# Stick-breaking attention in a transformer block: column sums on VectorE ahead of the product with minus ones

## The chip, the cores and the metric

The kernel runs on one core of a Trainium2 chip. The metric is the time of the whole program on the device, in microseconds; the program computes two transformer blocks of 512 tokens by 1024 channels in one launch, and the change touches one of the four mixers of the first.

## The reference

The stick-breaking mixer has 4 heads of 64 dimensions over 512 tokens. For a query i and the keys j before it:

```python
z = einsum('bqhd,bkhd->bhqk', q_blk, k) * scale
strict = kpos[None, :] < (t0 + arange(Q_BLOCK))[:, None]
log_1m = where(strict, log_sigmoid(-z), 0.0)
rem = cumsum(log_1m, axis=3, reverse=True) - log_1m
a = where(strict, exp(log_sigmoid(z) + rem), 0.0)
out = einsum('bhqk,bkhd->bqhd', a, v)
```

log_sigmoid(-z) is minus softplus(z), so log a is z minus the sum of softplus(z) over the key itself and all later keys that are still before the query.

## The kernel before, in words

Scores are held with keys on the partitions and queries on the free axis, in blocks of 128 keys. Key block kt has the queries from kt*128 on: 512, 384, 256 and 128 columns for kt = 0 to 3. They lie one behind another in the tile `sb_sp` (`sb_sp_t` in the profile), 1280 columns for each of two heads, at `SB_OFF` = 0, 512, 896, 1152. The heads go in two pairs (0, 1) and (2, 3), and the key blocks of a pair from the last to the first.

Three kinds of steps stand in the list `ORDER`, which all engines walk in the same order, each doing its own part of each step:
- `("sb_scores", pair, kt)`: TensorE multiplies keys by queries into a PSUM bank z(h,kt) and adds the causal mask through an identity (L1040 to L1052). ScalarE computes ln(1+exp(-|z|)) in three activations (L1479 to L1481). VectorE adds max(z, 0) and writes the softplus to `sb_sp` (L1963), which hands the bank back.
- `("sb_exp", pair, kt)`: TensorE takes the same bank over as r(h,kt) and adds to z the sum over later keys, with a minus sign (L1053 to L1064): for each later block j a product of the 128x128 matrix of minus ones (`sbm[:, 1]`) with the whole of block j's softplus, and for its own block a product with a triangular matrix (`sbm[:, 0]`). ScalarE takes the exponential into `sb_a` (L1489).
- `("sb_pv", pair)`: TensorE multiplies values by `sb_a`; ScalarE copies the result to `y[:, 6 + pair]`.

The core of the TensorE step is

```python
for j in range(NT - 1, kt, -1):
    mm(out[:, (j - kt) * P:w], sbm[:, 1], sb_sp[:, h % 2, SB_OFF[j]:SB_OFF[j] + T - j * P],
       False, False, skip_group_check=True)
last = mm(out[:, 0:w], sbm[:, 0], sb_sp[:, h % 2, SB_OFF[kt]:SB_OFF[kt] + w], False, True,
          skip_group_check=True)
```

All of it is in float32, where one matmul shows as two records in the profile. Matmuls are recorded at line L709 (a helper), transposes at L993.

These steps are woven by `plan()` between the attention steps of another mixer (`att_scores`, `att_norm`, `att_turn`, `att_pv` with units `("mla", head, query block)`), a projection in float32 halves (`fmk`, tiles `h_hi`, `h_lo`, `w_hi_t`, `w_lo_t`) and the output norms `("norm", ("y", g))` with `y_out(g)`. In the order of the list, what matters here is:

```
216 sb_scores 0,1   218 att_pv(0,1)  219 att_scores(2,0)  223 sb_exp 0,2  224 att_turn(0,3)
231 sb_scores 0,0   237 att_norm(2,2)  238 sb_exp 0,1   239 att_turn(2,1)  240 y_out 0
243 att_scores(2,3)  246 sb_scores 1,3   249 sb_exp 0,0   252 att_pv(2,2)   253 sb_pv 0
258 sb_scores 1,1   261 sb_scores 1,0   262 y_out 2   263 sb_exp 1,1   264 fmk wout k 0-1
265 sb_exp 1,0      266 fmk wout k 2    267 sb_pv 1   then y_out 3 and the rest of wout
```

(an attention step names one of its two heads.) A `y_out` on VectorE is six operations of 512 columns (L1572, L1636, L1640, twice). PSUM has eight banks, taken in the order in which they were filled; a taker waits until the last user has read it. GpSimd splits each weight tile into a high part (L2140) and a low part (L2142, `w_lo_t<-w_raw,w_hi_t`), as slots come free.

Of the kernel before, what the change touches and what calls it, by code (L numbers as in the profile page):

```python
# [19 lines left out]
ALU = mybir.AluOpType  # L20
# [5 lines left out]
P = 128  # L26
T = 512
NT = T // P
# [283 lines left out]
SEMAPHORES = """x_in0 x_in1 x_in2 x_in3 x_back ones_set r_cols mask_in mixer_in kv_in ksw_in kr_in zeros table_out sq_pe const_in wqb_in misc_in late_in alibi_in alibi_s bias_in y_out  # L312
w_hi wa_hi w_lo slot_used v_chain s_chain sq_s sq_v rstd rstd_used ms_lo
h_t h_hi u_hi h_ready x_pool p_chain bias_v bcast_v gate_v nsa_v cmpx cmp_s cmp_v att_l att_n att_exp att_p att_tr att_done
lora mla_k mla_q mla_rot sb_sp sb_exp sb_a sb_pe conv_y y_ready p_conv hid_s hid x_ready ret_s ret_a ret_d ret_done sil
o_ready m_ready gla_v gla_s gla_kd gla_st gla_a gla_done gla_t prod gate_s merged merged_hl q_s swa_s ft lo_t table last_t last_x""".split()


class Counts:
# [10 lines left out]
    def did(self, name, *key, by=1):  # L330
        self.n[name] = self.n.get(name, 0) + by
        assert (name, key) not in self.at, (name, key)
        self.at[(name, key)] = self.n[name]
        return self.sem[name], by

    def after(self, name, *key):
        v = self.at.get((name, key)) or self.known.get((name, key))
        assert v or not self.known, (name, key)
        return self.sem[name], v or 1
# [9 lines left out]
def _program(ctx, nc, a, known):  # L349
    C = Counts(known)  # L350
    did, after = C.did, C.after
# [38 lines left out]
    def sa(name, shape, dt=F32):  # L390
        return area.enter_context(nc.sbuf_tensor(name, shape, dt))
# [4 lines left out]
    y = sa("y", [P, KD, T])  # L396
# [8 lines left out]
    sbm = sa("sbm", [P, 3, P])  # L405
# [6 lines left out]
    nq, ks_d, kw_d, s_qk = x_sb[:, 0:2], x_sb[:, 2], x_sb[:, 3], x_sb[:, 4:8]  # L412

    cq, kr = y[:, 4:6], y[0:QKD, 6:8]
    conv_t = sa("conv_t_t", [P, 2, 32 + T])[:, :, 0:2 + T]
    cmp_pt = sa("cmp_pt_t", [P, NT, P])

# [39 lines left out]
    sb_sp = sn("sb_sp_t", [P, 2, 1280])  # L457
    sb_a = sn("sb_a_t", [P, 2, 1280])
# [31 lines left out]
    ret_a = sg("ret_a_t", [P, 1280])  # L490
    ret_d = att_pt
# [45 lines left out]
    def full(name):  # L537
        b, k = tenants[name]
        return C.sem[f"bank_full{b}"], k + 1

    def evacuated(name):
        b, k = tenants[name]
        return C.sem[f"bank_free{b}"], k + 1
# [130 lines left out]
    TAB = ((0, 512), (512, 128), (640, 512), (1152, 512))  # L674
    SB_OFF = [0, 512, 896, 1152]
    sb_order = [(2 * s[1] + hf, s[2]) for s in ORDER if s[0] == "sb_scores" for hf in range(2)]

    block = ctx.enter_context(nc.Block())

# [2 lines left out]
    def _(pe):  # L682
# [25 lines left out]
        def mm(out, lhs, rhs, start, stop, **kw):  # L708
            return pe.matmul(out, lhs, rhs, start=start, stop=stop, **kw)  # L709
# [55 lines left out]
        for step in ORDER:  # L765
            stage = step[0]
            if stage == "bias_tables":
# [3 lines left out]
                for n, (c0, w) in enumerate(TAB):  # L771
                    out = take(("tab", n))
# [3 lines left out]
            elif stage == "r_cols":  # L776
# [3 lines left out]
                out = take(("r_cols", key))  # L780
                for t in range(NT):
                    last = mm(out[:, t:t + 1], r_h[0:1, t * P:(t + 1) * P], ones[0:1, 0:1], True, True,
                              skip_group_check=True)
# [40 lines left out]
            elif stage == "fm" and step[1] not in TOGETHER:  # L824
                _, name, src = step
# [3 lines left out]
                out = take(name)  # L829
# [7 lines left out]
            elif stage == "tm":  # L837
                _, slot, name, cols, s, ns = step
# [23 lines left out]
            elif stage == "down":  # L862
                _, name, nk, o = step
# [4 lines left out]
                if nm == last_f:  # L868
                    tenants[nm] = tenants[("down2", 0, o)]
                    out = ps(nm)  # L870
                else:
                    out = take(nm)
                for k in range(nk):
# [4 lines left out]
                    if o == 0:  # L878
# [4 lines left out]
                               skip_group_check=both)  # L883
# [8 lines left out]
            elif stage == "cmp_up":  # L892
                _, name, kv, s = step
# [8 lines left out]
                for j in range(4 * s, 4 * s + 4):  # L902


                    c0 = 32 * j if kv == 0 else 512 + 32 * j - 96
# [7 lines left out]
            elif stage == "cmp_turn_h":  # L913

                for kv in range(2):
                    out = take(("cmp_h", kv))
# [6 lines left out]
            elif stage == "cmp_down":  # L923
# [3 lines left out]
                out = take("cmp_k")  # L927
# [3 lines left out]
                out = take("cmp_vt")  # L931
# [9 lines left out]
            elif stage == "cmp_bias":  # L941

                h = step[1]
                if h == 0:
                    take("cmp_bias")
                for qt in range(NT):
                    last = mm(ps("cmp_bias")[:, (qt * NH + h) * N_CMP:(qt * NH + h + 1) * N_CMP],
                              cb_t[:, h, qt * P:(qt + 1) * P], flip[0:N_CMP, P - N_CMP:P], True, True,
                              skip_group_check=True)
                if h == NH - 1:  # L950
                    fill("cmp_bias", last)
            elif stage == "cmp_scores":
# [5 lines left out]
                for qt in range(NT):  # L958
                    for j in range(2):
                        for hf in range(2):  # L960
# [3 lines left out]
                                      True, True, skip_group_check=True)  # L964
                            if (qt, j) == (NT - 1, 1):
                                fill(("cmp_sc", hf), last)
            elif stage == "cmp_turn":
                pe.wait_ge(*after("cmp_v", "p"))
                out = take("cmp_pt")
# [17 lines left out]
            elif stage == "att_turn":  # L987
                for u in step[1]:
                    A = att(u)
                    pe.wait_ge(*after("att_p", u))  # L990
                    out = take(("pt", u))
# [30 lines left out]
            elif stage == "mla_v":  # L1022
                pe.wait_ge(*after("rstd_used", "ckv"))
                pe.wait_ge(C.sem["wqb_in"], 16 * N_MLA)
                for n in range(2):
                    out = take(("mv", n))
                    for t in range(2):
                        tt = 2 * n + t
                        last = mm(out[:, t * 256:(t + 1) * 256], ckv[:, tt * P:(tt + 1) * P], wvb[:], True, True,
                                  skip_group_check=True)  # L1030
                    fill(("mv", n), last)
            elif stage == "mla_qk":
                h = step[1]
                out = take(("mk", h))
                fill(("mk", h), mm(out[0:QKD, :], wkb[:, h], ckv[:], True, True))
                pe.wait_ge(*after("rstd_used", "cq"))
                out = take(("mq", h))
                mm(out[0:QKD, :], wqb[:, 0, h], cq[:, 0], True, False)
                fill(("mq", h), mm(out[0:QKD, :], wqb[0:HD, 1, h], cq[0:HD, 1], False, True))
            elif stage == "sb_scores":  # L1040
                _, pair, kt = step
                pe.wait_ge(*evacuated("sk1"))
                pe.wait_ge(C.sem["mask_in"], 16 * N_MASK)
                for h in (2 * pair, 2 * pair + 1):
                    pb = HD * (h % 2)
                    out = take(("z", h, kt))
                    mm(out[:, 0:T - kt * P], s_qk[pb:pb + HD, 2 + pair, kt * P:(kt + 1) * P],
                       s_qk[pb:pb + HD, pair, kt * P:T], True, False, skip_group_check=True)
                for h in (2 * pair, 2 * pair + 1):

                    fill(("z", h, kt), mm(ps(("z", h, kt))[:, 0:P], ident[:], sbm[:, 2], False, False,
                                          skip_group_check=True), keep=True)  # L1052
            elif stage == "sb_exp":  # L1053

                _, pair, kt = step
                w = T - kt * P
                for h in (2 * pair, 2 * pair + 1):
                    out = take_over(("r", h, kt), ("z", h, kt))
                    for j in range(NT - 1, kt, -1):
                        mm(out[:, (j - kt) * P:w], sbm[:, 1], sb_sp[:, h % 2, SB_OFF[j]:SB_OFF[j] + T - j * P],  # L1060
                           False, False, skip_group_check=True)
                    last = mm(out[:, 0:w], sbm[:, 0], sb_sp[:, h % 2, SB_OFF[kt]:SB_OFF[kt] + w], False, True,
                              skip_group_check=True)
                    fill(("r", h, kt), last)  # L1064
            elif stage == "sb_pv":
                pair = step[1]
                out = take(("sb_o", pair))
                for h in (2 * pair, 2 * pair + 1):
                    pe.wait_ge(*evacuated(("r", h, 0)))
                for kt in range(NT):  # L1070
                    w = T - kt * P
# [5 lines left out]
            elif stage == "ret_scores":  # L1077
                _, h, jt = step
                pe.wait_ge(*evacuated(("rk", h)))
                out = take(("rs", h, jt))  # L1080
                fill(("rs", h, jt), mm(out[:, 0:T - jt * P], kf[:, h % 2, jt * P:(jt + 1) * P], qf[:, h % 2, jt * P:T],
                                       True, True))
            elif stage == "ret_pv":
                h = step[1]
                pe.wait_ge(*evacuated((("rv", h // 2), NT - 1)))
                pe.wait_ge(*evacuated(("rs", h, NT - 1)))
                for e in range(2):
                    out = take(("ret_o", h, e))
                    for jt in range(NT):
                        w = T - jt * P  # L1090
# [3 lines left out]
            elif stage == "ret_mean":  # L1094
                h = step[1]
                pe.wait_ge(*after("ret_s", h))
                fill(("mean", h), mm(take(("mean", h))[:], ones[:], tmp[:, 1], True, True))
            elif stage == "gla_decay":
                h = step[1]
                pe.wait_ge(*evacuated("ga"))  # L1100
                pe.wait_ge(C.sem["late_in"], 16 * 4)
                out = take(("gz", h))
                fill(("gz", h), mm(out[:], wa2[:, h * P:(h + 1) * P], ga_t[:], True, True))
            elif stage == "gla_turn":
                h = step[1]
                pe.wait_ge(*after("gla_v", "kd", h))
                out = take(("kdt", h))
# [3 lines left out]
                out = take(("ga_s", h))  # L1111
# [4 lines left out]
            elif stage == "gla_states":  # L1116
                h = step[1]
                pe.wait_ge(*evacuated(("kdt", h)))
                pe.wait_ge(*evacuated((("gv", h // 2), NT - 1)))
                for n in range(NGC - 1):  # L1120
                    out = take(("kv", h, n))
                    r = slice(GC * (n % 2), GC * (n % 2) + GC)
# [13 lines left out]
            elif stage == "gla_chunks":  # L1136
                h = step[1]
                pe.wait_ge(*evacuated(("ga_s", h)))
                for e in range(2):
                    out = take(("gla_o", h, e))  # L1140
                    for m in range(NT):
                        mm(out[:, m * P:(m + 1) * P], vt[:, m, h % 2 * 256 + e * P:h % 2 * 256 + (e + 1) * P], ga_m[:, m],
                           True, False, skip_group_check=True)
# [394 lines left out]
    def _(dve):  # L1538
# [6 lines left out]
        def own(name, *key):  # L1545
            dve.wait_ge(*after(name, *key))
# [44 lines left out]
        for step in ORDER:  # L1591
            stage = step[0]
# [7 lines left out]
            elif stage == "u":  # L1600

                _, key, c = step
# [11 lines left out]
            elif stage in ("apply_h", "y_out"):  # L1614
# [18 lines left out]
                for c in chunks:  # L1633
                    t = tmp[:, c % 2]
# [8 lines left out]
            elif stage == "fm":  # L1643
# [56 lines left out]
                elif key == "up1":  # L1700
                    _, half, c = name
# [8 lines left out]
                elif key in ("rg", "gg"):  # L1710
                    _, h, e = name
# [4 lines left out]
                elif key == "br":  # L1716

                    _, b, m = name
# [3 lines left out]
                    t = merged[:, m] if b == 0 else tmp[:, n % 2]  # L1722
# [231 lines left out]
            elif stage == "sb_scores":  # L1954
                _, pair, kt = step
                w = T - kt * P
                for h in (2 * pair, 2 * pair + 1):
                    n = sb_order.index((h, kt))
                    own("sb_exp", h, kt)
                    if h >= 2 and kt == NT - 1:  # L1960
                        dve.wait_ge(*full(("r", h - 2, 0)))
                    sp = sb_sp[:, h % 2, SB_OFF[kt]:SB_OFF[kt] + w]
                    dve.scalar_tensor_tensor(out=sp, in0=ps(("z", h, kt))[:, 0:w], scalar=0.0,  # L1963
                                             in1=sb_e[:, n % 2, 0:w], op0=ALU.max, op1=ALU.add)\
                       .then_inc(*release(("z", h, kt)))
                    dve.wait_ge(*evacuated(("z", h, kt)))
            elif stage == "ret_scores":
                _, h, jt = step
                w = T - jt * P
# [410 lines left out]
```

## Time and profile before

| | us |
|---|---|
| median of 3 runs | 1874.28 |
| lowest, highest | 1870.86, 1875.67 |
| profiled execution, its own time | 1876.29 |
| its span | 1874.5 |

In the profile TensorE is busy for 1826.0 us of the span (97%), VectorE for 826.7, ScalarE for 507.0 and GpSimd for 943.6. The mean granted clock of TensorE is 0.991. Read it with care: a busy TensorE is not TensorE at its peak, since matmuls overlap and the ends of their records are modelled; idle time of another engine costs nothing unless somebody waits for it. The steps of the stick-breaking mixer lie between 224 and 307 us.

### The profile page before, as it was taken

How to read it: one execution, taken by the hardware profiler on the slowest of the kernel's cores; microseconds unless marked ns; L12 is line 12 of the kernel's file. 1: busy time of each engine (PE TensorE's matmuls, PEld its weight loads, DVE VectorE, ACT ScalarE, POOL GpSimd, SP SyncE). 2: the span in 40 equal slices, each digit the busy share in tenths (PEclk: the TensorE clock that was granted, in tenths of full speed). 3: DMA queues.
4: the chain of work that ended last, by engine and by line, in shares of the span. 5: the costliest groups of instructions: out<-in, count | busy, mean ns of one | idle time of the engine just before them, and what ended most of it. 6: DMA issues, size and time to landing. Idle time of an engine off the chain costs nothing.

```text
span 1874.5 us, 22078 instructions
## 1 busy us (share of the span) xinstructions
PE 1826.0 (97%) x8488; PEld 1433.5 (76%) x8488; DVE 826.7 (44%) x1381; ACT 507.0 (27%) x1010; POOL 943.6 (50%) x510
## 2 busy tenths in 40 slices
PE   8998889999999999999999999999999999999998
PEld 5775556888888877777887888677778778888886
DVE  6327754531023232435103574666655675305533
ACT  3124654220012001212003232555400232212222
POOL 5442132766667665454664555443466545445442
PEclk9998999999999999999999999999999999999999
DMA  5610101332322232222322222212123222322321
GB/s 194 208 59 25 48 23 46 101 101 90 101 97 95 101 109 82 68 79 79 100 99 79 68 79 79 66 62 68 58 89 102 90 76 93 102 97 94 101 91 67
DMA packets 46728, 162.54 MB, mean 87 GB/s; under 512 B 5392, under 2 KB 6736, under 8 KB 46241
## 3 DMA queue, kind: packets, MB, share of 16 engines
q1 hardware_dynamic: 43088, 154.52, 24.7%
q10 hardware_dynamic: 3537, 6.61, 1.2%
q8 instruction: 69, 1.13, 0.3%
q14 instruction: 34, 0.28, 0.0%
HBM read 158.13 MB, written 2.12 MB: 85 GB/s over the span
## 4 chain that ended last, share of the span: by engine, by line
PE 89%; DVE 6%; ACT 3%; issue 1%; POOL 1%; DMA 1%; ACTq 0%; SPq 0%; DVEq 0%; POOLq 0%
PE bank L709 87%; PE bank L993 1%; DVE att_l_t L1911 1%; DVE att_l_t L1891 1%; DVE o_hi L1550 0%; POOL w_lo_t L2142 0%; ACT sq L1208 0%; DVE o_lo L1551 0%; DMA x_sb<-in_x 0%; ACT att_l_t L1441 0%; DVE h_lo L1607 0%; ACT sb_e L1480 0%; ACT att_pt L1453 0%; DVE att_l_t L1913 0%; ACT h_hi L1274 0%
## 5 line engine op out<-in xcount | busy, mean ns | idle before, releaser
L2142 POOL TENSOR_TENSOR w_lo_t<-w_raw,w_hi_t 128x1024 fp32r<-128x1024 f32 x276 | 691.6, 2506 | 188.2 <-ACT w_hi_t L1257 170.1
L2140 POOL TENSOR_SCALAR w_hi_t<-w_raw 128x1024 fp32r<-128x1024 f32 x216 | 235.0, 1088 | 674.5 <-PE bank L709 653.1
L709 PE MATMUL bank<-h_hi,w_hi_t 128*128 128x512 f32 x1088 | 446.5, 410 | 17.9 <-ACT h_hi L1274 12.8
L709 PE MATMUL bank<-h_hi,w_lo_t 128*128 128x512 f32 x1088 | 428.2, 394 | 0.0
L709 PE MATMUL bank<-h_lo,w_hi_t 128*128 128x512 f32 x1088 | 419.4, 392 | 0.7 <-DVE h_lo L1607 0.5
L709 PEld LDWEIGHTS bank<-h_hi,w_hi_t 128*128 128x128 f32 x1088 | 207.1, 190 | 81.5 <-issue 35.1
L709 PEld LDWEIGHTS bank<-h_lo,w_hi_t 128*128 128x128 f32 x1088 | 205.5, 189 | 48.0 <-issue 2.9
L709 PEld LDWEIGHTS bank<-h_hi,w_lo_t 128*128 128x128 f32 x1088 | 207.0, 190 | 42.8 <-issue 1.2
L709 PE MATMUL bank<-hid_hi,w_hi_t 128*128 128x512 f32 x432 | 168.0, 389 | 0.0
L709 PE MATMUL bank<-hid_lo,w_hi_t 128*128 128x512 f32 x432 | 168.0, 389 | 0.0
L709 PE MATMUL bank<-hid_hi,w_lo_t 128*128 128x512 f32 x432 | 168.0, 389 | 0.0
L1257 ACT ACTIVATE w_hi_t<-w_raw 128x1024 fp32r<-128x1024 f32 x60 | 63.6, 1060 | 219.9 <-PE bank L709 219.8
L709 PE MATMUL bank<-u_hi,w_hi_t 128*128 128x512 f32 x256 | 100.0, 391 | 0.0
L709 PE MATMUL bank<-u_hi,w_lo_t 128*128 128x512 f32 x256 | 99.6, 389 | 0.0
L709 PE MATMUL bank<-u_lo,w_hi_t 128*128 128x512 f32 x256 | 99.6, 389 | 0.0
L709 PEld LDWEIGHTS bank<-hid_hi,w_lo_t 128*128 128x128 f32 x432 | 81.1, 188 | 16.9
L709 PEld LDWEIGHTS bank<-hid_lo,w_hi_t 128*128 128x128 f32 x432 | 81.1, 188 | 16.9
L709 PEld LDWEIGHTS bank<-hid_hi,w_hi_t 128*128 128x128 f32 x432 | 81.1, 188 | 16.8
L709 PE MATMUL bank<-o_hi,w_hi_t 128*128 128x512 f32 x192 | 78.7, 410 | 1.9 <-DVE o_lo L1551 1.9
L1322 ACT ACTIVATE r<-r 128x512 f32<-128x512 f32 x32 | 20.2, 632 | 215.0 <-DVE r L1706 215.0
L1441 ACT ACTIVATE att_l_t<-att_l_t,small 128x256 f32<-128x256 f32 (+3 forms) x112 | 57.3, 512 | 77.8 <-DVE small L1895 47.0
L1706 DVE SCALAR_TENSOR_TENSOR r<-bank,r_h 128x512 f32<-128x512 f32 x32 | 22.1, 692 | 123.5 <-PE bank L709 119.2
(291 smaller groups left out, 2621.2 us busy)
## 6 DMA issues: line engine op xcount, KB each, us to landing
w_raw<-in_w SPq DMA_DIRECT2D x276, 512.0 KB, 3.2
y<-in_w SPq DMA_DIRECT2D x6, 512.0 KB, 5.2
x_sb<-in_x SPq DMA_DIRECT2D x4, 512.0 KB, 7.3
x_sb<-in_x ACTq DMA_DIRECT2D x2, 1024.0 KB, 5.3
out_y<-x_sb SPq DMA_DIRECT2D x8, 256.0 KB, 2.1
u_raw<-in_w SPq DMA_DIRECT2D x2, 512.0 KB, 5.9
toep<-table ACTq DMA_DIRECT2D x4, 256.0 KB
decay<-in_decay SPq DMA_DIRECT2D x1, 1024.0 KB, 4.7
```

The source lines that it names most:

```text
L709: return pe.matmul(out, lhs, rhs, start=start, stop=stop, **kw)
L993: last = pe.transpose(out[:, b * P:(b + 1) * P], att_l[:, att_at[u] % 4, b * P:(b + 1) * P], ident[:])
L1257: act.activation(w_hi[:, RING[i]], w_raw[:, n % RAW], ACT.Copy).then_inc(*did("wa_hi", i))
L1322: chain(act.activation(r1[:, n % 2], r1[:, n % 2], ACT.Square))
L1441: act.activation(L, L, ACT.Exp, bias=sm[:, 1:2], accum_out=sm[:, 2:3]).then_inc(*did("att_exp", u))
L1706: dve.scalar_tensor_tensor(out=r1[:, n % 2], in0=ps(name)[:], scalar=0.0, in1=r_h[:], op0=ALU.max, op1=ALU.mult).then_inc(*release(name))
L1891: dve.tensor_tensor_reduce(L, ps(("sc", u))[:, 0:A["w"]], A["bias"], 1.0, -3.0e38, ALU.add, ALU.max, sm[:, 0:1]).then_inc(*release(("sc", u)))
L1911: dve.tensor_scalar(L, L, sm[:, 3:4], A["gate"], ALU.mult, ALU.mult).then_inc(*did("att_p", u))
L2140: pool.tensor_scalar(hi, raw, 1.0, 0.0, ALU.mult, ALU.add).then_inc(*did("w_hi", i))
L2142: pool.tensor_tensor(lo, raw, hi.bitcast(F32), ALU.subtract).then_inc(*did("w_lo", i))
```

## The change

VectorE adds softplus blocks of the same query block, so that TensorE multiplies each query column of a key block by minus ones once. The sums, 256 columns per head, lie in `y[:, 7]`, which is not in use until the result of `sb_pv` 1. For kt = 1 the matrix meets block 2's first 128 columns and the sum of blocks 2 and 3 for the last query block; for kt = 0 it meets block 1's first 128 columns and a sum of 256 columns (blocks 1+2 and 1+2+3). Two semaphores are new, `sb_sum` and `sb_two`. TensorE waits for `sb_sum` ahead of the product with minus ones in the steps kt = 1 and kt = 0; VectorE waits in step `sb_exp` kt = 1 until r(h,1) is filled, since it overwrites the sum that this step reads.

```diff
+    sb_sums = y[:, 7].rearrange("p (h t) -> p h t", h=2)
...
+    def sb_keys(h, kt):
+
+        sp = lambda j, c0, w: sb_sp[:, h % 2, SB_OFF[j] + c0:SB_OFF[j] + c0 + w]
+        sums = sb_sums[:, h % 2]
+        return {2: [(P, sp(3, 0, P))], 1: [(P, sp(2, 0, P)), (2 * P, sums[:, P:2 * P])],
+                0: [(P, sp(1, 0, P)), (2 * P, sums)]}[kt]
...
                     out = take_over(("r", h, kt), ("z", h, kt))
-                    for j in range(NT - 1, kt, -1):
-                        mm(out[:, (j - kt) * P:w], sbm[:, 1], sb_sp[:, h % 2, SB_OFF[j]:SB_OFF[j] + T - j * P],
-                           False, False, skip_group_check=True)
+                    if kt < NT - 1:
+                        pe.wait_ge(*(after("sb_sum", h, kt) if kt < 2 else evacuated(("z", h, 3))))
+                        for c0, keys in sb_keys(h, kt):
+                            mm(out[:, c0:c0 + keys.shape[-1]], sbm[:, 1], keys, False, False, skip_group_check=True)
...
+                for h in (2 * pair, 2 * pair + 1):
+                    sums = sb_sums[:, h % 2]
+                    of = lambda j, c0: sb_sp[:, h % 2, SB_OFF[j] + c0:SB_OFF[j] + c0 + P]
+                    if kt == 2:
+                        dve.tensor_tensor(sums[:, P:2 * P], of(2, P), of(3, 0), ALU.add).then_inc(*did("sb_sum", h, 1))
+                    elif kt == 1:
+                        dve.tensor_tensor(sums[:, 0:P], of(1, P), of(2, 0), ALU.add).then_inc(*did("sb_two", h))
+            elif stage == "sb_exp":
+                _, pair, kt = step
+                for h in (2 * pair, 2 * pair + 1) if kt == 1 else ():
+                    dve.wait_ge(*full(("r", h, 1)))
+                    own("sb_two", h)
+                    own("sb_sum", h, 1)
+                    dve.tensor_tensor(sb_sums[:, h % 2, P:2 * P], sb_sums[:, h % 2, P:2 * P],
+                                      sb_sp[:, h % 2, SB_OFF[1] + 2 * P:SB_OFF[1] + 3 * P], ALU.add)\
+                       .then_inc(*did("sb_sum", h, 0))
```

The first VectorE part belongs to the step `sb_scores` and stands behind both heads' softplus.

## Rows read from the trace of the kernel before

**Rows 1.** The page: its head and the chain that ended last, shares by engine.

```profile
span 1874.5 us, 22078 instructions
...
PE 89%; DVE 6%; ACT 3%; issue 1%; POOL 1%; DMA 1%; ACTq 0%; SPq 0%; DVEq 0%; POOLq 0%
```

**Rows 2.** Timeline of PE: E(0,1), E(1,0). Columns: start, us, engine, line, operation.

```profile
261.13 2.77 PE L709 MATMUL bank<-sb_sp_t,sbm 128*128 128x128 f32 x12
...
298.51 4.48 PE L709 MATMUL bank<-sb_sp_t,sbm 128*128 128x128 f32 x16
```

**Rows 3.** Groups by line and form, 224 to 304 us; then timeline of DVE with idle.

```profile
L1963 DVE SCALAR_TENSOR_TENSOR sb_sp_t<-bank,sb_e 128x128 f32<-128x128 f32 x4 | 1.2, 292 | 5.5 <-PE bank L709 3.5 <-ACT sb_e L1481 2.0
...
233.14 0.56 DVE L1891 CUSTOM_DVE_ANT_0 att_l_t<-bank,causal 128x384 f32<-128x384 f32 x1 [0.80 <-PE bank L709]
...
288.34 0.69 DVE L1567 TENSOR_TENSOR sq_sum<-sq 128x512 f32<-128x512 f32 x1 [1.89 <-ACT sq L1208]
...
294.93 0.69 DVE L1963 SCALAR_TENSOR_TENSOR sb_sp_t<-bank,sb_e 128x512 f32<-128x512 f32 x1 [3.04 <-ACT sb_e L1481]
```

**Rows 4.** Timeline around 249.75 us: PE, POOL, DVE.

```profile
248.11 1.47 PE L709 MATMUL bank<-sb_sp_t,sbm 128*128 128x128 f32 x8
...
249.57 2.37 POOL L2142 TENSOR_TENSOR w_lo_t<-w_raw,w_hi_t 128x1024 fp32r<-128x1024 f32 x1
249.75 0.29 DVE L1891 CUSTOM_DVE_ANT_0 att_l_t<-bank,causal 128x128 f32<-128x128 f32 x1
...
250.19 1.11 PE L993 MATMUL bank<-ident,att_l_t 128*128 128x128 f32 x8 [0.61 <-DVE small L1891]
```

**Rows 5.** Timeline of VectorE beside GpSimd at 322 us; VectorE alone at 1035 us.

```profile
321.90 2.40 POOL L2142 TENSOR_TENSOR w_lo_t<-w_raw,w_hi_t 128x1024 fp32r<-128x1024 f32 x1
...
322.37 2.48 DVE L1607 SCALAR_TENSOR_TENSOR u_lo<-x_sb,par,u_hi 128x512 fp32r<-128x512 f32 x1 [0.86 <-ACT u_hi L1274]
...
1035.01 0.68 DVE L2058 TENSOR_TENSOR kf<-kf,att_l_t 128x512 f32<-128x512 f32 x1
```

**Rows 6.** Timeline 268 to 273.2 us: PE and DVE.

```profile
268.07 1.19 PE L709 MATMUL bank<-sq_sum,ones 128*128 128x512 f32 x2 [2.18 <-DVE sq_sum L1567]
...
268.56 0.42 DVE L1913 TENSOR_SCALAR att_l_t<-att_l_t,small 128x384 f32<-128x384 f32 x1
...
272.46 0.69 DVE L1891 CUSTOM_DVE_ANT_0 att_l_t<-bank,causal 128x512 f32<-128x512 f32 x1
...
273.17 0.53 PE L709 MATMUL bank<-x_sb 64*128 64x128 f32 x4
```

**Rows 7.** Timeline of ACT at 282.49 us.

```profile
282.49 1.08 ACT L1453 ACTIVATE att_pt<-bank 128x512 f32<-128x512 f32 x2 [2.41 <-PE bank L709]
```

**Rows 8.** Timeline of DVE: last softplus add, last operation of y_out(2).

```profile
296.74 0.69 DVE L1963 SCALAR_TENSOR_TENSOR sb_sp_t<-bank,sb_e 128x512 f32<-128x512 f32 x1 [1.12 <-ACT sb_e L1481]
...
300.32 0.69 DVE L1640 TENSOR_TENSOR h_lo<-tmp,h_hi 128x512 fp32r<-128x512 f32 x1
```

**Rows 9.** Windows: length, then PE, PEld, DVE, ACT, POOL busy, PEclk, DMA share, GB/s.

```profile
230.00:232.00 2.00, 0.88 (x4) 0.37 (x2) 0.57 (x3) 1.91 (x7) 0.00 (x0) 1.00 0.00 0
...
268.00:270.00 2.00, 1.93 (x4) 0.92 (x5) 1.90 (x5) 1.18 (x3) 0.00 (x0) 0.74 0.00 0
270.00:272.00 2.00, 2.00 (x4) 0.81 (x3) 1.97 (x5) 0.63 (x1) 0.00 (x0) 0.50 0.00 0
272.00:274.00 2.00, 2.00 (x14) 1.29 (x13) 1.93 (x6) 0.62 (x1) 0.00 (x0) 0.91 0.00 0
...
1492.00:1494.00 2.00, 0.00 (x0) 0.00 (x0) 0.96 (x2) 0.94 (x2) 1.31 (x1) 1.00 0.00 0
1494.00:1496.00 2.00, 0.45 (x1) 0.48 (x2) 1.97 (x4) 0.72 (x1) 0.00 (x0) 0.58 0.79 240
1496.00:1498.00 2.00, 2.00 (x6) 1.52 (x6) 1.97 (x4) 0.72 (x1) 0.00 (x0) 0.50 0.06 23
...
1500.00:1502.00 2.00, 2.00 (x8) 1.61 (x7) 1.97 (x4) 0.73 (x1) 0.00 (x0) 0.71 0.00 0
```

More of the change, by code:

```diff
@@ L314 @@
 h_t h_hi u_hi h_ready x_pool p_chain bias_v bcast_v gate_v nsa_v cmpx cmp_s cmp_v att_l att_n att_exp att_p att_tr att_done
-lora mla_k mla_q mla_rot sb_sp sb_exp sb_a sb_pe conv_y y_ready p_conv hid_s hid x_ready ret_s ret_a ret_d ret_done sil
+lora mla_k mla_q mla_rot sb_sp sb_sum sb_two sb_exp sb_a sb_pe conv_y y_ready p_conv hid_s hid x_ready ret_s ret_a ret_d ret_done sil
 o_ready m_ready gla_v gla_s gla_kd gla_st gla_a gla_done gla_t prod gate_s merged merged_hl q_s swa_s ft lo_t table last_t last_x""".split()
```

## The prediction

> **What bounds the kernel now.** I read the page first: one chain, 89% of it TensorE, over a span of 1874.5 us [rows 1]. That is an average, so it says nothing of the stretch in which the change lies. I then took the timeline of 224 to 310 us, the only stretch in which the softplus tile is touched, and looked in it for three things: how long TensorE spends in each of the eight steps "sb_exp", who waits where just behind each of them, and where VectorE has room. The reader is to see that in this stretch TensorE is not the bound all the time: before 250.19 it stood idle for 0.61 us, before 268.07 for 2.18 us [rows 4, 6], while ScalarE and VectorE worked through attention and norms. From 268 to 282 us, and again from 289 to 307 us, it works almost without a break. After 316 us the program is dense matmul, and whatever delay stands there is carried to the end.
>
> The profiled execution took 1876.29 us, 2.0 above the median of 1874.28; the three runs lie between 1870.86 and 1875.67. Every term below is a difference inside that profiled execution, so I add the sum to the median. About 0.3%, 5.6 us, is what a measurement of this kernel can tell from no change.
>
> **What is removed.** Let E(p,k) be the step "sb_exp" of head pair p and key block k, S(p,k) its "sb_scores". E(p,3) is unchanged; E(p,2) keeps its one product with minus ones per head. E(p,1) goes from 128+256 to 128+128 columns of that product, E(p,0) from 128+256+384 to 128+256 in two matmuls in place of three. With the own-block product, E(p,1) had 2x768=1536 columns in 2.77 us, E(p,0) 2x1280=2560 in 4.48 us [rows 2]; E(0,0) is of the same make. (4.48-2.77)/1024 = 1.67 ns a column. So E(p,1) loses 256 columns or 0.43 us, E(p,0) 768 columns or 1.28 us; over both pairs 3.4 us of TensorE. That is the most it can give, and it is 0.18% of the time.
>
> **What is added.** Twelve VectorE adds of 128 columns, three per head. The nearest row is the 128-column operation on the same tile, 292 ns [rows 3]; two heads make about 0.6 us with their gaps. By place:
> - Behind S(0,2) and S(1,2), four adds, and behind S(1,1), two. VectorE then sat idle for 0.80, 1.89 and 3.04 us [rows 3]. Cost nothing; without that cover 0.6 us each.
> - Behind S(0,1), two adds, at 249.75. This is site A.
> - In E(0,1), two adds, behind the normalization of attention unit (2,2) at 268.98. This is site C.
> - In E(1,1), two adds, which wait until TensorE has filled r(h,1), but stand in VectorE's queue behind the whole of y_out(2). This is site E.
>
> **Site A.** At 249.75 VectorE starts the reduction for scores (mla 2,0), and TensorE's transposes wait for the bank that it frees, until 250.19 [rows 4]. Two adds of 0.29 put there would delay it by 0.55 us. But both inputs of the adds lie in SBUF, and GpSimd's low-part subtraction runs from 249.57 to 251.94 [rows 4]. The trace shows what such a pair does: at 322.37, a VectorE operation with two wide SBUF inputs begun during the same GpSimd subtraction (321.90 to 324.30) lasted 2.48 us and ended 0.55 behind it; a two-input operation of that width with GpSimd idle took 0.68 us [rows 5]. So the first add ends at about 252.1, the second at 252.4, and the reduction starts 2.65 us late. I take 2.65; the ends are 0.55 and 2.65. By the Trainium skill, page "SBUF — State Buffer", section "Who interferes with whom", an instruction of VectorE with two SBUF inputs and a GpSimd instruction that reads SBUF take the same read interface, and the one that starts first blocks the other to its end. By that rule the site costs the 2.65, by the plain duration 0.55; rows 5 side with the rule. All that follows hangs on TensorE's restart (scores, attention values, the square sums of norm y0, then ScalarE's softplus for S(0,0)), so all of it moves.
>
> **E(0,1).** The 0.43 us saved lies ahead of an idle time of 2.18 us that a square sum from ScalarE and VectorE ends at 268.07 [rows 6]. Worth nothing.
>
> **Site C.** VectorE runs without a gap from the end of that normalization at 268.98 through y_out(0) to the reduction of scores (2,3), 272.46 to 273.15, whose bank the second matmul of S(1,3) takes at about 273.3 [rows 6]. The adds move that by 0.55 and leave TensorE waiting about 0.45. Ends: 0 and 0.6. GpSimd rests there. The sums are then ready five microseconds before E(0,0) wants them.
>
> **E(0,0).** TensorE goes on without a wait from 273.17 [rows 6] through E(0,0) to the attention product that releases ScalarE at 282.49, after 2.41 us of idleness of ScalarE [rows 7]. The saving of 1.28 us counts in full: -1.28. Next in line are the two exponentials of r(·,0), which follow 1.28 earlier with it.
>
> **Site E.** Before, E(1,0) ran from 298.51 to 302.99 [rows 2]. Now it waits for the last adds. VectorE ends the softplus add of S(1,0) at 297.43, does y_out(2) until 301.01 [rows 8], and only then the add for h=2: done at 301.30, TensorE starts about 0.15 later (as after 250.04 in rows 4), 301.45. With 4.48-1.28=3.20 us it ends at 304.65, so +1.66 in place of -1.28. The 0.43 of E(1,1) only makes the wait longer: TensorE stands from 298.08 to 301.45, 3.4 us. Behind it in TensorE's queue are the third k-chunk of the output projection, the value product, and through that norm y3, on which everything later depends. The second head's add is hidden under the first head's matmuls.
>
> **The clock.** Sites A and E each leave TensorE idle for over 3 us (A: from 248.11+1.47=249.58 to 252.84). Behind the 2.18 us of idleness before 268.07 the granted clock fell to 0.5, that is 1.2 of 2.4 GHz, for 0.52/0.5+2+0.18x2=3.4 us; behind the empty stretch 1492 to 1494 for 0.84/0.5+2+2+0.58/0.5=6.8 us (of the two whole windows one stands), of which 5.6 us were worked. Behind a half empty stretch at 230 it stayed at 1.00 [rows 9]. Work at half clock loses half its time: 1.7 to 2.8 us a spell. Site E lies in dense work: 2.3, the middle. At site A a third of the following time is ScalarE's and VectorE's: 1.5. Ends 0 and 3 each.
>
> **Sum.** A 2.65+1.5, C 0.45, E(0,0) -1.28, E 1.66+2.3: +7.3 us, 1881.6 us.
>
> **The rivals.**
> - GpSimd does not block the adds, or VectorE comes first: A costs 0.55 and its idleness is 1.2 us, too short for the clock. 0.55+0.45-1.28+1.66+2.3=+3.7, 1878.0. For it: the margin is 0.18 us (249.57 against 249.75). Against: rows 5. 0.17.
> - The clock holds at both places: 2.65+0.45-1.28+1.66=+3.5, 1877.8; at one of them, +5 to +6. For it: falls depend on where the idle time lies. Against: every idle time over 2 us that I saw in the timeline was followed by one. 0.15.
> - Not slower: the sums are ready whenever TensorE wants them, and it is the bound throughout: -3.4, 1870.9. It decides at E(1,0): the last add must be done before 298.08, while y_out(2) holds VectorE to 301.01. For it speaks only the 89% of the chain. 0.05; it would itself be within 0.3% more often than not.
>
> **How the numbers follow.** The forecast has 0.60, of which some 0.08 ends below 5.6 us by its unknown clock terms and the scatter of the runs; 0.03 is left for dearer clock spells. Slower 0.55, same 0.42, faster 0.03. The range reaches from the two middle rivals, less a microsecond or two of scatter, to the forecast with both clock spells dear and site C in full: 1876 to 1887.
>
> **What would show it.** In the changed profile: 8480 TensorE matmul records for 8488 and twelve more VectorE operations; at about 249.75 an add of over 2 us beside GpSimd's subtraction, and TensorE idle there for 3 us; near 300 TensorE idle for over 3 us, released by VectorE's add; granted clock below 1.00 behind both; E(p,0) in 3.2 us at full clock. I am wrong if the add at 249.75 takes 0.3 us, if the wait before E(1,0) is short, or if the later stretch takes the delay back.

## The result and the profile after

| | before | after |
|---|---|---|
| median of 10 runs, us | 1874.58 | 1881.06 |
| lowest, highest | 1870.86, 1876.11 | 1878.57, 1885.74 |
| ratio, 95% interval | | 1.0039, 1.0026 to 1.0052 |
| profiled execution, its span | 1874.5 | 1883.5 |

The kernel became slower by 0.39%, where 1881.6 us was forecast. The profiled execution of after is one of the slow ones of its ten (1885.27 us), so its rows show each step, but its clock terms lie at the upper end. The page of after, as [rows 1] of before (columns: busy us, share, instructions; then the chain):

```profile
span 1883.5 us, 22088 instructions
...
PE 1828.1 (97%) x8480; PEld 1433.6 (76%) x8480; DVE 830.6 (44%) x1393; ACT 507.6 (27%) x1010; POOL 944.4 (50%) x510
...
PE 88%; DVE 7%; ACT 3%; issue 2%; DMA 0%; POOL 0%; ACTq 0%; SPq 0%; DVEq 0%; POOLq 0%
```

Eight matmul records fewer and twelve VectorE operations more, as the change says. VectorE's share of the chain rose from 6 to 7%. On so broad a view no more can be seen; the shares hide a matter of 6 us in 1880.

**Site A**, the timeline of after that answers to [rows 4]:

```profile
247.85 1.47 PE L717 MATMUL bank<-sb_sp_t,sbm 128*128 128x128 f32 x8
...
249.31 2.34 POOL L2167 TENSOR_TENSOR w_lo_t<-w_raw,w_hi_t 128x1024 fp32r<-128x1024 f32 x1
249.49 2.51 DVE L1982 TENSOR_TENSOR y<-sb_sp_t 128x128 f32<-128x128 f32 x2
251.92 0.28 DVE L1900 CUSTOM_DVE_ANT_0 att_l_t<-bank,causal 128x128 f32<-128x128 f32 x1
...
252.35 1.94 PE L1001 MATMUL bank<-ident,att_l_t 128*128 128x128 f32 x8 [3.03 <-DVE small L1900]
```

Two adds of 128 columns take 2.51 us; elsewhere in this kernel two take 0.49. The first of them lasts 2.30 us, to 251.79; the second ends at 252.00. GpSimd's subtraction ended at 249.31+2.34=251.65. TensorE's idle time grew from 0.61 to 3.03 us. The transposes behind it take 1.94 us in place of 1.11, at a granted clock of 0.50 (windows below).

**Site C and E(0,0)**, the timeline as [rows 6, 7]:

```profile
274.69 1.19 PE L717 MATMUL bank<-sq_sum,ones 128*128 128x512 f32 x2 [2.18 <-DVE sq_sum L1576]
...
275.52 0.49 DVE L1989 TENSOR_TENSOR y<-y,sb_sp_t 128x128 f32<-128x128 f32 x2
...
281.89 0.49 PE L717 MATMUL bank<-sb_sp_t,sbm 128*128 128x128 f32 x2
...
288.23 1.09 ACT L1462 ACTIVATE att_pt<-bank 128x512 f32<-128x512 f32 x2 [2.41 <-PE bank L717]
```

Against before the square sum is 6.62 us late (274.69 for 268.07), E(0,0) 7.03 (281.89 for 274.86), ScalarE's copy 5.74 (288.23 for 282.49). So site C costs 0.41 and E(0,0) gives back 1.29.

**Site E**, as [rows 8] and E(1,0) of [rows 2]:

```profile
302.50 0.69 DVE L1972 SCALAR_TENSOR_TENSOR sb_sp_t<-bank,sb_e 128x512 f32<-128x512 f32 x1 [1.19 <-ACT sb_e L1490]
...
306.08 0.69 DVE L1649 TENSOR_TENSOR h_lo<-tmp,h_hi 128x512 fp32r<-128x512 f32 x1
306.80 0.49 DVE L1989 TENSOR_TENSOR y<-y,sb_sp_t 128x128 f32<-128x128 f32 x2
307.24 0.76 PE L717 MATMUL bank<-sb_sp_t,sbm 128*128 128x128 f32 x2 [3.28 <-DVE y L1989]
...
311.64 1.76 PE L717 MATMUL bank<-sb_sp_t,sbm 128*128 128x512 f32 x2
```

The last adds stand behind y_out(2), TensorE waits 3.28 us for them, and E(1,0) then lasts to 313.40, 10.41 us later than before (302.99). ScalarE's copy stood 5.74 us later than before; the rest, 4.67 us, is what site E takes in this execution.

The windows, as [rows 9] (length, PE, PEld, DVE, ACT, POOL busy, granted clock, DMA):

```profile
250.00:252.00 2.00, 0.00 (x0) 0.00 (x0) 2.00 (x3) 0.00 (x0) 1.65 (x1) 0.92 0.38 152
252.00:254.00 2.00, 1.65 (x8) 1.57 (x8) 1.86 (x10) 1.52 (x6) 0.00 (x0) 0.50 0.67 215
...
262.00:264.00 2.00, 2.00 (x6) 0.50 (x5) 0.00 (x0) 0.00 (x0) 0.00 (x0) 0.50 0.00 0
264.00:266.00 2.00, 1.70 (x17) 1.46 (x16) 0.00 (x0) 0.20 (x2) 0.00 (x0) 0.67 0.00 0
...
306.00:308.00 2.00, 0.76 (x3) 0.79 (x4) 1.23 (x4) 0.00 (x0) 0.00 (x0) 0.57 0.00 0
308.00:310.00 2.00, 2.00 (x5) 1.15 (x4) 0.00 (x0) 0.00 (x0) 0.00 (x0) 0.50 0.00 0
310.00:312.00 2.00, 2.00 (x6) 1.44 (x5) 0.00 (x0) 0.60 (x1) 0.00 (x0) 0.50 0.00 0
312.00:314.00 2.00, 2.00 (x6) 0.98 (x5) 0.00 (x0) 0.57 (x1) 0.00 (x0) 0.72 0.00 0
```

Behind site A the clock stayed at half from about 251.7 to 265.3 us, 13.6 us; behind site E from 306.3 to 313.1, 6.8 us. The span grew by only 9.0: elsewhere in this execution other low spells are missing or shorter. Such a spell lay at 1371 in before and none lies there in after; the one near 1495 [rows 9] had lasted 6.8 us and lasts 3.4 in after. In the other kernels' profiles, too, these spells come and go.

### The profile page after: what moved, and what is told of

It is laid out like the page before. It is cut to its first block, busy times and chain, and to the rows that moved or that the text cites. A ratio compares the mean times of both kernels' runs of the same rounds, so it can differ in the third digit from the quotient of the medians.

```text
span 1883.5 us, 22088 instructions
## 1 busy us (share of the span) xinstructions
PE 1828.1 (97%) x8480; PEld 1433.6 (76%) x8480; DVE 830.6 (44%) x1393; ACT 507.6 (27%) x1010; POOL 944.4 (50%) x510
## 4 chain that ended last, share of the span: by engine, by line
PE 88%; DVE 7%; ACT 3%; issue 2%; DMA 0%; POOL 0%; ACTq 0%; SPq 0%; DVEq 0%; POOLq 0%
PE bank L717 87%; PE bank L1001 1%; DVE sq_sum L1576 1%; DVE att_l_t L1920 1%; DVE h_lo L1616 1%; DVE o_hi L1559 1%; DVE att_l_t L1900 1%; DVE tmp L1581 0%; ACT sq L1217 0%; DVE o_lo L1560 0%; ACT sb_e L1489 0%; DMA x_sb<-in_x 0%; ACT att_l_t L1450 0%; ACT sb_e L1488 0%; POOL w_lo_t L2167 0%
```

## The experiments

Four kernels change the place or the kind of the adds, three more take the change apart, three settle the rest. Each is compared with runs of the kernel before on its own chip, so the ratios are the measure. A ratio need not be the quotient of the two medians, and medians of different series are only roughly comparable. I number the sites as the prediction does.

| kernel | what it has | median us | ratio to before, 95% interval |
|---|---|---|---|
| after | sites A, C, E | 1881.06 | 1.0039 (1.0026 to 1.0052) |
| x1_site_a | C, E | 1875.10 | 1.0005 (0.9996 to 1.0014) |
| x2_site_e | A, C | 1877.10 | 1.0010 (1.0000 to 1.0020) |
| x11_site_e_again | A, C | 1875.74 | 1.0012 (1.0003 to 1.0022) |
| x3_psum | A with one SBUF input, C, E | 1875.61 | 1.0008 (0.9998 to 1.0017) |
| x4_both | none | 1871.40 | 0.9981 (0.9972 to 0.9989) |
| x8_fill_both | A, C, E, waits filled | 1878.32 | 1.0027 (1.0018 to 1.0035) |
| x6_mm_only | fewer columns, no adds | 1871.69 | 0.9982 (0.9973 to 0.9990) |
| x7_adds_only | adds, old matmuls | 1878.24 | 1.0021 (1.0011 to 1.0031) |
| x9_fill_a | A filled, C | 1874.69 | 1.0002 (0.9993 to 1.0011) |
| x10_site_c | C | 1872.77 | 0.9987 (0.9979 to 0.9996) |

### Site A taken away: x1_site_a

```diff
             elif stage == "sq":
+                if step[1:] == (("y", 1), 1):
+                    for h in (0, 1):
+                        dve.tensor_tensor(sb_sums[:, h, 0:P], sb_sp[:, h, SB_OFF[1] + P:SB_OFF[1] + 2 * P],
+                                          sb_sp[:, h, SB_OFF[2]:SB_OFF[2] + P], ALU.add).then_inc(*did("sb_two", h))
                 squares(*step[1:])
...
-                    elif kt == 1:
+                    elif kt == 1 and pair == 1:
```

> The two adds of blocks 1 and 2 of pair 0 no longer stand behind S(0,1) (site A) but ahead of the square sum of norm y1, where VectorE had 1.66 us of idle time and GpSimd rests. Theory (blocked add, idle TensorE, clock): the add of 2.3 us and TensorE's wait of 3.0 us behind E(0,2) are gone, no spell of low clock begins near 251, and the time falls by 2.4 us and the spell's 1.7 to 4.4 us, to 1875 to 1877. Rival (site A is a side matter, the wait ahead of E(1,0) is nearly all of the loss): less than 2 us gained, 1879 to 1881.

Measured: 1875.10 us, 6 us under the changed kernel. TensorE's wait behind E(0,2) is back to 0.61 us and no low spell begins there. Site A, with all that it drags along, is about six tenths of the whole swing of 9.7 us between after and x4_both. The median hides two groups: five of the eleven runs took 1873.3 to 1874.1 us and five 1877.8 to 1879.2; the profile is of the first group (1874.05 us). It shows the moved adds, which still read two SBUF inputs, while GpSimd rests (busy for 0.00 us from 264 to 266), and it has a surprise at site E. Its timeline, then its windows:

```profile
264.71 0.49 DVE L1610 TENSOR_TENSOR y<-sb_sp_t 128x128 f32<-128x128 f32 x2
...
299.83 0.46 PE L717 MATMUL bank<-sb_sp_t,sbm 128*128 128x128 f32 x2 [3.26 <-DVE y L1993]
...
302.07 1.02 PE L717 MATMUL bank<-sb_sp_t,sbm 128*128 128x512 f32 x2
```

```profile
296.00:298.00 2.00, 0.57 (x3) 0.15 (x1) 1.97 (x4) 0.00 (x0) 0.00 (x0) 1.00 0.00 0
298.00:300.00 2.00, 0.17 (x1) 0.20 (x2) 1.82 (x5) 0.00 (x0) 0.00 (x0) 1.00 0.00 0
300.00:302.00 2.00, 2.00 (x10) 1.45 (x10) 0.00 (x0) 0.38 (x1) 0.00 (x0) 1.00 0.00 0
```

TensorE waits 3.26 us, for 3.28 in after, and the clock stays at 1.00: E(1,0) takes 303.09-299.83=3.26 us, where it took 6.16 in after. x3_psum, below, has site E too, and there a wait of 3.24 us was likewise followed by a clock of 1.00. So the wait brought the low spell in one of three profiles.

### Site E taken away: x2_site_e and x11_site_e_again

```diff
     run(sbs[cut:cut + 1] + sqs(("y", 2), 2) + sbs[cut + 1:cut + 3] + [("norm", ("y", 2))] + sbs[cut + 3:cut + 4] +
-        [("y_out", 2)] + sbs[cut + 4:-2])
+        sbs[cut + 4:-2] + [("y_out", 2)])
```

> y_out(2) stands behind sb_exp 1,1 in the list, so VectorE makes the last two adds of pair 1 ahead of its six operations. Theory: TensorE's wait of 3.3 us ahead of E(1,0) is gone, and so is the low clock behind it; against the changed kernel 1.7+1.3+2.9 us less, about 1875. Rival (site A is nearly all of it, E's wait only moves idle time from norm y3): 1879 to 1881.

> x2_site_e once more, on the same chip as x9_fill_a, to compare with it. Theory: 1876 to 1878 as the first time, with a spell of low clock in some of its runs longer than in others, so runs from 1873 to 1881. Rival (the first series was an accident of its chip): under 1875.

Measured: 1877.10 and 1875.74. E(1,0) follows the adds with no wait worth a row. The gain is 4.0 and 5.3 us by the medians, 5.4 and 5.1 by the ratios, where 5.9 was expected: 1875 was the sum with a low spell of 2.9 us taken away in full. That the average over runs has less of it fits x1_site_a, but was not measured. The second series gave the same ratio within its interval, with a median just under the 1876 to 1878 expected. At site A the two profiles differ: TensorE waits 3.03 us in both, in x2_site_e a low spell of 10.2 us begins about 5.6 us behind the restart, in x11_site_e_again none does.

### One SBUF input at site A: x3_psum

```diff
...
+                    elif kt == 1 and pair == 0:
+                        dve.tensor_tensor(sums[:, 0:P], ps(("z", h, 1))[:, P:2 * P], of(2, 0), ALU.max)\
+                           .then_inc(*release(("z", h, 1)))
                     elif kt == 1:
                         dve.tensor_tensor(sums[:, 0:P], of(1, P), of(2, 0), ALU.add).then_inc(*did("sb_two", h))
...
```

The rest of the edit moves the signal that hands the bank back from the softplus to this operation, and lets the add of site C wait for it.

> At site A the two operations read z from its PSUM bank in place of the softplus of block 1, and take the larger of the two in place of the sum, so the values of pair 0 are not the attention's; place, width and count are those of the change. Theory (two SBUF inputs are blocked by GpSimd's subtraction): 0.3 us each, TensorE's wait there about 1.2 us in place of 3.0, no spell of low clock there, 1876 to 1878. Rival (any VectorE operation at that place is held up, or the adds wait for a semaphore): again over 2 us, TensorE idle for 3 us, time as the changed kernel, 1881.

Its timeline at the same place:

```profile
250.29 2.36 POOL L2175 TENSOR_TENSOR w_lo_t<-w_raw,w_hi_t 128x1024 fp32r<-128x1024 f32 x1
250.47 0.49 DVE L1985 TENSOR_TENSOR y<-bank,sb_sp_t 128x128 f32<-128x128 f32 x2
250.87 0.28 DVE L1900 CUSTOM_DVE_ANT_0 att_l_t<-bank,causal 128x128 f32<-128x128 f32 x1
...
251.31 1.11 PE L1001 MATMUL bank<-ident,att_l_t 128*128 128x128 f32 x8 [1.00 <-DVE small L1900]
```

The pair starts 0.18 us behind the same GpSimd subtraction, as in after, and takes 0.49 us in place of 2.51. The first input moved to PSUM, and the sum became a maximum; a sum of two SBUF inputs takes the same 0.49 us per pair where GpSimd rests (x1_site_a), so it is not the kind of operation. It takes both, two SBUF inputs and GpSimd's subtraction; place, width and wait for a semaphore are not the cause. TensorE waits 1.00 us, and the time falls to 1875.61, a little under the 1876 expected.

### Everything in its gap: x4_both

```diff
-        [("y_out", 2)] + sbs[cut + 4:-2])
+        sbs[cut + 4:-2] + [("y_out", 2)])
...
+                if step[1:] == (("y", 1), 1):
+                    for h in (0, 1):
+                        dve.tensor_tensor(sb_sums[:, h, 0:P], sb_sp[:, h, SB_OFF[1] + P:SB_OFF[1] + 2 * P],
+                                          sb_sp[:, h, SB_OFF[2]:SB_OFF[2] + P], ALU.add).then_inc(*did("sb_two", h))
+                    for h in (0, 1):
+                        dve.wait_ge(*full(("r", h, 1)))
+                        own("sb_two", h)
+                        own("sb_sum", h, 1)
+                        dve.tensor_tensor(sb_sums[:, h, P:2 * P], sb_sums[:, h, P:2 * P],
+                                          sb_sp[:, h, SB_OFF[1] + 2 * P:SB_OFF[1] + 3 * P], ALU.add)\
+                           .then_inc(*did("sb_sum", h, 0))
...
-                    elif kt == 1:
+                    elif kt == 1 and pair == 1:
...
-                for h in (2 * pair, 2 * pair + 1) if kt == 1 else ():
+                for h in (2 * pair, 2 * pair + 1) if kt == 1 and pair == 1 else ():
```

> All four adds of blocks 1 to 3 of pair 0 ahead of the square sum of norm y1 (sites A and C empty), and y_out(2) behind sb_exp 1,1 (site E empty). Theory: all twelve adds are hidden; what is left is the saving of TensorE, 1.28 at E(0,0) and 0.43+1.28 at pair 1: 3.0 us under the kernel before, 1871.6. Rival (the saved matmul time is given back to the latency of ScalarE and VectorE): 1874 to 1875.

Measured: 1871.40, 0.19% under the kernel before (interval 0.11 to 0.28%). This version beats both. By the ratio it gains 3.6 us, where the TensorE time that the change saves was put at 3.0 of use and 3.4 in all. Its timeline:

```profile
266.03 0.48 DVE L1610 TENSOR_TENSOR y<-sb_sp_t 128x128 f32<-128x128 f32 x2
266.43 0.49 DVE L1616 TENSOR_TENSOR y<-y,sb_sp_t 128x128 f32<-128x128 f32 x2
267.76 0.69 DVE L1576 TENSOR_TENSOR sq_sum<-sq 128x512 f32<-128x512 f32 x1 [0.85 <-ACT sq L1217]
...
296.71 0.49 DVE L2000 TENSOR_TENSOR y<-y,sb_sp_t 128x128 f32<-128x128 f32 x2
297.30 0.39 PE L717 MATMUL bank<-sb_sp_t,sbm 128*128 128x128 f32 x2
```

The four adds of pair 0 fit into VectorE's idle time, of which 0.85 us is left; the last two are done at 297.20, and E(1,0) starts at 297.30.

### Fewer columns alone, adds alone: x6_mm_only and x7_adds_only

```diff
-        return {2: [(P, sp(3, 0, P))], 1: [(P, sp(2, 0, P)), (2 * P, sums[:, P:2 * P])],
-                0: [(P, sp(1, 0, P)), (2 * P, sums)]}[kt]
+        return {2: [(P, sp(3, 0, P))], 1: [(P, sp(2, 0, P)), (2 * P, sp(2, P, P))],
+                0: [(P, sp(1, 0, P)), (2 * P, sp(1, P, 2 * P))]}[kt]
...
-                        pe.wait_ge(*(after("sb_sum", h, kt) if kt < 2 else evacuated(("z", h, 3))))
```

Both edits are against after. x6_mm_only also leaves out all twelve adds. x7_adds_only has the old loop over j in TensorE's step with all adds in place; its only wait for a sum stands ahead of the last value product.

> The fewer columns alone: no adds and no waits for them; in place of the sums the product with minus ones reads softplus columns of the same width, so the values of rem are not the attention's. Theory (the saving is 1.28+0.43+1.28 us, E(0,1)'s 0.43 is hidden): 1871.6, as x4_both. Rival (freed TensorE time is given back to ScalarE and VectorE): 1873.5 to 1875.

> The twelve adds alone: TensorE multiplies the old 1280 columns per head and waits for no sum, except ahead of the last value product, where the sums have long been there. Theory: site A is all there (blocked add, 3.0 us of idle TensorE, low clock behind it) and site C, site E costs nothing: 2.4+0.45 and a clock term of 1.7 to 4.4 above the kernel before, 1879.5 to 1882. Rival (the waits for the sums are what costs): 1875 to 1876.

Fewer columns alone give 1871.69 and a ratio of 0.9982, with x4_both at 0.9981: in x4_both the adds cost nothing that these runs can tell. The adds alone cost 3.4 us by the medians, 3.9 by the ratio, although TensorE waits for no sum while it could be late. At 1878.24 that is under the 1879.5 expected. The clock term was smaller here, at least in the profile: the low spell behind the blocked add lasted 3.4 us, not 13.6. The rival's 1875 to 1876 lies under all nine runs (1876.42 at the lowest).

### The idle time filled: x8_fill_both and x9_fill_a

```diff
+                if step[1][0] == ("mla", 0, 3):
+                    pe.wait_ge(*evacuated(("z", 0, 1)))
+                    for n in range(4):
+                        mm(ps(("z", 0, 1))[:, 0:384], ident[:], causal[:, 0:384], False, False, skip_group_check=True)
...
+                if (pair, kt) == (1, 0):
+                    spare = take(("sb_o", 1))
+                    for n in (T, T, T, T // 2):
+                        mm(spare[:, 0:n], ident[:], causal[:, 0:n], True, True)
```

> The changed kernel, with matmuls that add nothing while TensorE waits: four of 384 columns of zeros added to z(0,1) ahead of the transposes at site A (2.6 us of a wait of 3.0), and 1792 columns into the bank of the value product, written over later, ahead of E(1,0) (3.0 us of 3.3). Both waits stay. Theory (half of the loss at site A is the spell of low clock behind the idle time): no low clock behind 250 and 300, the time falls by 3 to 5 us, to 1876 to 1878, and the runs lie closer together than 1878.6 to 1885.7. Rival (the clock is a by-product; the waits alone cost the 6.5 us): 1881.

> As x2_site_e (no wait ahead of E(1,0)), and the four empty matmuls of 384 columns in TensorE's wait at site A. What is left is the blocked add itself, 2.4 us, and site C's 0.4, over the 1871.5 of x4_both and x6_mm_only. Theory (the spell of low clock behind site A was the other half of x2_site_e's 5.7 us): 1874 to 1875, that is 2 to 3 us under x2_site_e. Rival (x2_site_e's time had another cause further on): 1877.

Timeline of x8_fill_both, then its windows behind site A and at site E:

```profile
248.60 2.74 PE L717 MATMUL bank<-causal,ident 128*128 128x384 f32 x8
248.76 2.35 POOL L2175 TENSOR_TENSOR w_lo_t<-w_raw,w_hi_t 128x1024 fp32r<-128x1024 f32 x1
248.93 2.52 DVE L1990 TENSOR_TENSOR y<-sb_sp_t 128x128 f32<-128x128 f32 x2
...
251.81 1.11 PE L1005 MATMUL bank<-ident,att_l_t 128*128 128x128 f32 x8 [0.46 <-DVE small L1908]
```

```profile
252.00:254.00 2.00, 2.00 (x22) 1.57 (x21) 1.73 (x8) 1.59 (x7) 0.00 (x0) 1.00 0.84 270
...
302.00:304.00 2.00, 1.77 (x8) 1.27 (x9) 0.28 (x2) 0.00 (x0) 0.00 (x0) 1.00 0.00 0
```

The add is blocked as before, TensorE merely does not rest, and the transposes are back to 1.11 us at a clock of 1.00. The time fell by 2.7 us by the medians (2.2 by the ratios, whose intervals overlap) to 1878.32, with runs from 1877.25 to 1881.63, just above the 1876 to 1878 expected. x9_fill_a does this at site A alone and with site E away: 1874.69. By the medians that is 1.0 us under x11_site_e_again and 2.4 under x2_site_e, by the ratios 1.9 and 1.5, at or under the lower end of the 2 to 3 us expected; the intervals overlap here too.

The profiles say what the clock cost behind site A, from the start of the transposes to the square sum of norm y1:

| kernel | TensorE's wait | transposes start | square sum starts | between | low clock in between |
|---|---|---|---|---|---|
| before | 0.61 | 250.19 | 268.07 | 17.88 | none |
| after | 3.03 | 252.35 | 274.69 | 22.34 | 13.6 |
| x2_site_e | 3.03 | 251.68 | 272.37 | 20.69 | 10.2 |
| x7_adds_only | 3.03 | 253.20 | 272.38 | 19.18 | 3.4 |
| x11_site_e_again | 3.03 | 251.34 | 269.22 | 17.88 | none |
| x8_fill_both | 0.46, the rest filled | 251.81 | 269.69 | 17.88 | none |
| x9_fill_a | 0.46, the rest filled | 252.62 | 272.09 | 19.47 | 3.4 |

So the same wait of 3.03 us cost 4.46, 2.81, 1.30 and 0.00 us of clock. In x9_fill_a the clock stood at 1.00 through the filled wait, yet a spell began about 6 us behind it, in the stretch where that of x2_site_e began:

```profile
256.00:258.00 2.00, 1.08 (x3) 0.26 (x4) 1.19 (x5) 0.75 (x2) 0.00 (x0) 1.00 0.00 0
258.00:260.00 2.00, 2.00 (x6) 1.03 (x7) 1.62 (x8) 1.20 (x4) 0.00 (x0) 0.66 0.02 4
```

And x11_site_e_again kept 1.00 with no filling at all. That filling is what holds the clock is therefore likely from the times, but not shown by single profiles.

### Site C alone: x10_site_c

It is x1_site_a and the edit of x2_site_e together.

> As x4_both, but the last two adds of pair 0 stand again ahead of y_out(0), at site C; nothing else waits. Theory: TensorE loses 0.4 us there, 1871.8; too small for the interval, so the profile decides: S(1,3)'s second matmul 0.4 us later behind the square sum than in x4_both. Rival (site C is hidden by the low clock that TensorE has there anyway): no shift.

In x10_site_c the first product with a sum in E(0,0) stands at 275.10, 7.53 us behind the square sum at 267.57; in x4_both at 275.71, 7.11 us behind 268.60. That is 0.42 us, as after showed. The medians, 1872.77 and 1871.40, agree in sign and cannot tell more. The two rows of x10_site_c, then those of x4_both:

```profile
267.57 1.10 PE L717 MATMUL bank<-sq_sum,ones 128*128 128x512 f32 x2 [2.18 <-DVE sq_sum L1576]
275.10 0.60 PE L717 MATMUL bank<-y,sbm 128*128 128x256 f32 x2
...
268.60 1.22 PE L717 MATMUL bank<-sq_sum,ones 128*128 128x512 f32 x2 [2.18 <-DVE sq_sum L1576]
275.71 0.60 PE L717 MATMUL bank<-y,sbm 128*128 128x256 f32 x2
```

### The clock across runs

Every run has its mean granted clock. In after, the four runs at 0.992 to 0.991 with the shortest times took 1878.6 to 1878.7 us, two at 0.990 took 1882.0, and three at 0.988 to 0.987 took 1885.1 to 1885.7; one more at 0.992 took 1880.15. The same instructions are 7 us apart. 0.0045 of 1880 us is 8.5 us of full clock given away, which is enough for the whole spread. In x2_site_e it runs from 1873.3 at 0.994 to 1880.7 at 0.988. The kernel before spans 1871.0 to 1877.4 over 0.994 to 0.991, but its runs at 0.994 alone lie at 1871.0 to 1871.6 and at 1873.5 to 1874.8, so something besides the mean clock, where 0.001 is 1.9 us, moves its time too; what, no run here shows.

## Why the prediction was right, point by point

- **The saving.** Forecast 1.28 at E(0,0), 0.43+1.28 at pair 1, E(0,1) worth nothing. After shows 1.29 at E(0,0). From the end of the last softplus add to the end of E(1,0) it was 5.56 us before and is 300.49-296.68=3.81 in x4_both, so 1.75 at pair 1. E(0,1)'s columns left the way to the square sum at 17.88 us wherever the clock held (table above), so they were worth nothing. x6_mm_only shows 3.2 us in all by its medians and 3.4 by its ratio, for 3.0 forecast.
- **Hidden adds.** Six were costed at nothing; x4_both shows that even all twelve can be hidden.
- **Site A, the blocked add.** Forecast 2.65. The reduction that the adds delay started at 251.92, where the length of the adds alone would have put it at about 249.9, and TensorE's idle time grew by 2.42 us. x3_psum shows the cause. The first add ended 0.14 us behind GpSimd's subtraction, for 0.16 forecast; the forecast then gave the second add 0.3 us ahead of the reduction, while in the rows these operations overlap and the reduction starts 0.13 us behind the first add's end. The Trainium skill says, on "SBUF — State Buffer", section "Who interferes with whom", that a VectorE instruction with two SBUF inputs and a GpSimd instruction that reads SBUF contend, and that whichever starts first holds the other up for its whole instruction. The trace agrees: GpSimd started 0.18 us ahead of the add and the pair took 2.51 us, beside 0.49 with one SBUF input.
- **Site A, the clock.** Forecast 1.5, ends 0 and 3. The profiled execution of after paid 4.46 us, beyond the upper end; with x2_site_e, x7_adds_only and x11_site_e_again, which have the same wait, it is 4.46, 2.81, 1.30 and 0.00, on average 2.1. Over the runs x9_fill_a puts it at 1.5 to 1.9 us by the ratios, 1.0 to 2.4 by the medians.
- **Site C.** Forecast 0.45, measured 0.41 and 0.42.
- **Site E, the wait.** Forecast: TensorE stands for 3.4 us and E(1,0) ends 1.66 later. From the end of the last softplus add to the end of E(1,0) it was 5.56 us before and 303.09-295.78=7.31 in x1_site_a, where the clock held: 1.75. The wait was 3.26 to 3.28.
- **Site E, the clock.** Forecast 2.3. In after E(1,0) took 6.16 us in place of 3.26, a term of 2.90; in x1_site_a and x3_psum it took 3.26, a term of nothing. By the ratios site E without site A costs 3.4 us (x1_site_a less x10_site_c), which is already the price of the wait, 1.75 behind where it was and 1.75 of saving forgone. The prediction gave as its reason that every idle time over 2 us was followed by a fall; that held in one execution and not beyond it, as these two profiles and x11_site_e_again's site A show. So the split of the clock's 3.8 us between A and E was not right as it stood, and that their sum fits is in part luck.
- **The sum.** +7.3 forecast; +6.5 by the medians, +7.3 by the ratio (0.0039 of 1874.6), with an interval of 4.9 to 9.7. The terms without the clock come to 2.42+0.41-1.29+1.75=3.3 as measured, for 3.5 forecast, which leaves 3.2 to 4.0 for the clock, for 3.8 forecast. The rivals: an unblocked add is refuted by the row; a clock that holds at both places may be true of the runs near 1878.6, of which no profile was taken, and x8_fill_both puts it at 1878.3, close to its 1877.8; sums that are ready in time are true only once the adds are moved, in x4_both.

What stays open: the two sites together cost more than each alone. By the ratios E costs 3.4 us without A (x1_site_a less x10_site_c), and 5.1 to 5.4 with it (after less x11_site_e_again and x2_site_e). The intervals are about 2 us wide each, so it may be chance; whether low spells follow each other more readily was not tried.

## What to carry to other kernels

Work moved from a bound engine to an idle one is free only where it lies in that engine's queue in a real gap: look at what the consumer waits for just behind the chosen place, and at what stands ahead of the last add of a chain. Here two edits of place, with not one instruction less, turned +0.4% into -0.2%. Before putting a VectorE operation with two SBUF inputs anywhere, look at what GpSimd is doing in those microseconds; and price a wait on TensorE as its length plus, in some runs, a spell at half clock.

## What the runs showed of the hardware that was not expected

- A wait of TensorE of 3.26 us was followed by no low clock at all (x1_site_a), one of 3.24 us neither (x3_psum), and one of 3.28 us in the same place by 6.8 us of it (after). A wait of 2.17 to 2.18 us ahead of norm y1's square sum was followed by a spell of 3.4 us in every profile read here but that of x2_site_e; there the wait was 2.06 us, and the spell began some 5 us later and lasted 6.8.
- The length of a low spell varies as much as its coming: behind the same wait of 3.03 us at site A it lasted 13.6 us (after) and 3.4 us (x7_adds_only), in x2_site_e 10.2 us began 5.6 us later, and in x11_site_e_again there was none.
- Matmuls by an identity, of zeros at site A and of the causal mask at site E, kept TensorE busy and the granted clock at 1.00 through both waits (x8_fill_both). That they were the reason is likely and not shown, since the clock also held in waits without them.
